# First attention of a two-block model: another order for VectorE's row maxima, taps, halves and weight splits, and two modulation rows taken ahead of the exponentials

## The reference

```python
def hybrid_mixer(h, w_in, b_f, conv_w, conv_b, conv_ln_g, conv_ln_b, w_o):
    q, k, v, f_logit, conv_val, conv_gate = jnp.split(h @ w_in, splits, axis=-1)
    log_f = jax.nn.log_sigmoid(f_logit + b_f)
    attn = fox_attention(q, k, v, log_f)          # 8 heads of 64, causal, softmax over rows
    u = conv_val * jax.nn.sigmoid(conv_gate)
    u = causal_depthwise_conv(u, conv_w, conv_b)  # 31 taps, 512 channels
    u = jax.nn.silu(layer_norm(u, conv_ln_g, conv_ln_b))
    return jnp.concatenate([attn, u], axis=-1) @ w_o

# fox_attention, per block of 128 queries:
#   s = q k^T / sqrt(64) + cum[t] - cum[s], masked to s <= t;  p = softmax(s);  out = p v
# ahead of it: mod = silu(c) @ ada_w + ada_b (shifts, scales and gates of every norm)
# after it: x + g1 * rms_norm(y), then a SwiGLU feed-forward, then the second block
```

## Time and profile before

| | us |
|---|---|
| median of three runs | 1454.34 |
| the profiled execution: its time | 1453.96 |
| its span, first to last instruction | 1452.2 |
| TensorE busy, of the span | 1364.5 |
| VectorE busy | 820.9 |
| ScalarE busy | 589.0 |
| GpSimd busy | 409.3 |
| mean granted TensorE clock | 0.967 of full |

### The profile page before, as it was taken

The page is one execution under the profiler, slowest core; times in us unless marked ns, Lnnn a source line. Parts: engine busy times, 40 slices in busy tenths (PEclk is TensorE's granted clock), DMA queues, the critical chain, the costliest instruction groups (busy, mean ns, idle before and its releaser), DMA issues. The chain is left out here.

```text
span 1452.2 us, 19530 instructions
## 1 busy us (share of the span) xinstructions
PE 1364.5 (94%) x7904; PEld 1080.3 (74%) x7904; DVE 820.9 (57%) x965; ACT 589.0 (41%) x848; POOL 409.3 (28%) x191
## 2 busy tenths in 40 slices
PE   5999789969999999999999998998999999999996
PEld 3777566748888888887778886766777799777775
DVE  3788763476556555333755665776842831565544
ACT  4323445442222222212454346776632422455541
POOL 0000000018987888999200000000000050232220
PEclk9999889979999999999799999999999999999998
DMA  9433035213544545554132333334132342111121
GB/s 390 148 145 117 30 109 182 66 51 120 215 186 166 186 167 222 204 182 174 58 120 87 114 109 105 117 102 151 38 110 88 127 163 88 58 47 42 59 88 58
DMA packets 41350, 181.12 MB, mean 125 GB/s; under 512 B 3392, under 2 KB 20160, under 8 KB 21312
## 3 DMA queue, kind: packets, MB, share of 16 engines
q1 hardware_dynamic: 40128, 171.73, 32.9%
q10 hardware_dynamic: 1152, 8.39, 1.7%
HBM read 173.75 MB, written 6.36 MB: 124 GB/s over the span
## 5 line engine op out<-in xcount | busy, mean ns | idle before, releaser
L193 DVE TENSOR_TENSOR wlo<-raw,whi 128x2048 fp32r<-128x2048 f32 x95 | 253.7, 2670 | 182.2 <-ACT whi L189 179.6
L200 POOL TENSOR_TENSOR ada_raw<-ada_raw,cs 128x2048 f32<-128x2048 f32 x36 | 150.1, 4171 | 504.2 <-DVE h2lo L451 457.5
L271 PE MATMUL ps<-hhi,whi 128*128 128x512 f32 x640 | 252.1, 394 | 2.3 <-PEq L562 0.8
L271 PE MATMUL ps<-hhi,wlo 128*128 128x512 f32 x640 | 249.4, 390 | 0.0
L271 PE MATMUL ps<-hlo,whi 128*128 128x512 f32 x640 | 249.1, 389 | 0.0
L189 ACT ACTIVATE whi<-raw 128x2048 fp32r<-128x2048 f32 x95 | 181.5, 1911 | 143.6 <-PE ps L1303 91.3
L209 POOL TENSOR_TENSOR ada_raw<-ada_raw 128x1024 f32<-128x1024 f32 x72 | 164.4, 2283 | 5.7
L271 PEld LDWEIGHTS ps<-hhi,whi 128*128 128x128 f32 x640 | 120.2, 188 | 28.7 <-issue 2.4
L271 PEld LDWEIGHTS ps<-hhi,wlo 128*128 128x128 f32 x640 | 120.1, 188 | 25.7
L271 PEld LDWEIGHTS ps<-hlo,whi 128*128 128x128 f32 x640 | 120.2, 188 | 24.3
L2030 POOL TENSOR_TENSOR x<-x,rest 128x256 f32<-128x256 f32 (+3 forms) x32 | 49.0, 1531 | 163.8 <-DVE rest L2325 163.8
(11 more groups left out here) (373 smaller groups left out, 2810.1 us busy)
## 6 DMA issues: line engine op xcount, KB each, us to landing
raw<-panels SPq DMA_DIRECT2D x87, 1024.0 KB, 4.9
ada_raw<-ada SPq DMA_DIRECT2D x48, 1024.0 KB, 6.7
first<-ada SPq DMA_DIRECT2D x8, 1024.0 KB, 20.7
bc<-ac_rows SPq DMA_DIRECT2D x32, 256.0 KB, 3.8
raw<-panels ACTq DMA_DIRECT2D x8, 1024.0 KB, 5.1
x_kept<-x SPq DMA_DIRECT2D x2, 2048.0 KB, 9.6
x<-x_kept SPq DMA_DIRECT2D x2, 2048.0 KB, 8.0
x<-x_in SPq DMA_DIRECT2D x1, 2048.0 KB, 9.1
```

Of the source, the lines that this page charges most:

```text
L193: e.tensor_tensor(wlo[:, c % 2, :, :], raw[:, c % 2, :, :], whi[:, c % 2, :, :].bitcast(F32), ALU.subtract).then_inc(lo_split, 1)
L200: e.tensor_tensor(ada_raw[:, c % 2, :, :], ada_raw[:, c % 2, :, :], cs[:, which, :].unsqueeze(2).to_broadcast([P, KT, 256]), ALU.mult).the ...
L271: mm = e.matmul(ps[:, 2 * (qc % 2) + b, :], w[:, c % 2, 2 * k + b, :], src[part][:, k, :], **flags)
```

## The change

It reorders one block's programs and adds no arithmetic:

- In dense step 5, VectorE writes `ncx` ahead of the step's ten taps, not behind them.
- In dense step 6, the split of panel 8 is taken out; it now follows the row maximum of unit 0.
- In the units, VectorE's row maximum and the reciprocal come first; then `out_lo`; then a split if one is due (`SPLIT_AT`: panels 8, 9, 10, 11 in units 0, 7, 9, 12); then the taps; and last `take_half`, which no longer splits.
- On ScalarE, in units 11 and 12, the first `ada_keep` comes ahead of the exponentials. Units 13 and 14 stay.

```diff
@@ ScalarE, units @@
                             if n >= 7 and n % 4 == 3:
                                 out_hi((n - 7) // 4)
+                            if n in (11, 12):
+                                ada_keep(act, ROWS_AT[n][0], MODB, 256)
                             if n < NU:
...
-                            if n in ROWS_AT:
+                            if n in (13, 14):
                                 ada_keep(act, ROWS_AT[n][0], MODB, 256)
@@ VectorE, dense steps @@
-                            split_lo(dve, s + 2, 0)
+                            if s < DENSE - 1:
+                                split_lo(dve, s + 2, 0)
...
-                            conv_taps(dve, done_taps, done_taps + DENSE_TAPS[s])
-                            done_taps += DENSE_TAPS[s]
                             if s == 5:
                                 dve.wait_ge(A["nc_hi"], 2)
                                 for r0 in (0, HD):
                                     dve.tensor_tensor(ncx[r0 + 32:r0 + 32 + H1, :], ncum,
                                                       ncx[0:H1, :].bitcast(F32), ALU.subtract).then_inc(A["nc"], 1)
+                            conv_taps(dve, done_taps, done_taps + DENSE_TAPS[s])
+                            done_taps += DENSE_TAPS[s]
@@ VectorE, units @@
-                            if b == 1:
-                                split_lo(dve, c + 2, 0)
+
+                        SPLIT_AT = {0: DENSE + 1}
+                        SPLIT_AT.update({n + 1: HALVES[H][1] + 2 for n, H in HALF_AT.items() if HALVES[H][2] == 1})
...
                         for n in range(NU + 3):
-                            if n >= 7 and n % 4 == 3:
-                                out_lo((n - 7) // 4)
                             if n < NU:
                                 dve.wait_ge(A["s_done"], n + 1)
...
-                            if n in HALF_AT:
-                                take_half(HALF_AT[n])
+                            if n >= 7 and n % 4 == 3:
+                                out_lo((n - 7) // 4)
+                            if n in SPLIT_AT:
+                                split_lo(dve, SPLIT_AT[n], 0)
                             if n == 15:
                                 read_mod(dve, 8, 20)
...
+                            if n in HALF_AT:
+                                take_half(HALF_AT[n])
```

## The result

The changed kernel takes 1438.01 us, the median of four runs (1437.19 to 1440.56); beside them the kernel before took 1453.96 us. The ratio is 0.9888, with a 95% interval of 0.9873 to 0.9902, so 16 us are gone, clear of noise. The forecast was 1437.5 us, in a range of 1429 to 1446.

A forecast was written before the change was run, and what follows sets the result against it. TensorE was held up by VectorE, late by order, not load, in the first attention's units. Terms -20.0 (waits), +3.0 (half clock) and +0.6 (end) sum to -16.4 us from 1453.96: 1437.5 us, range 1429 to 1446.

The forecast's parts named there:

- Start: Before unit 0: ncx ends at 120.4, not 127.1, so unit 0's logits start 1.56 us earlier, at 125.8.
- Units 0 to 4: New 2.6 us idle before the second maximum, then halves no longer wait; unit 4's logits at 145.7, 3.8 us ahead.
- Units 4 to 8: TensorE is the bound again: four units in 21.3 us, unit 8's logits at 167.0, 11.1 us ahead.
- close meeting: Unit 8: panel 9's split ends about 167.7, v pieces need it at 168.0; priced at nothing, up to 1 us if late.
- Units 8 to 12: 26.4 us, kept-row waits of 0.4 and 1.1 replacing 3.48; unit 12's logits at 193.4, 20.0 us ahead.
- Units 12 to 15: Load a16 goes out behind w13, TensorE idles 2.8 us; 23.5 us in all, unit 15's logits at 216.9.
- Half clock: TensorE at 1.2 GHz: 7 of 28 us reached the end before; 3 us of the 7 left after the change.
- the walk: Stepping the engines' programs unit by unit at full clock; the old order gives unit 15's logits at 230, trace 236.94.
- End: Unit 15: read_mod now stands behind out_lo(2), adding 0.6 us to TensorE's existing 1.56 us wait.
- the lower bound: No half clock, a16 in time, units 2 us shorter: stated as -24.5 us, 1429.5 us.
- the rivals: Half clock stays or grows (chance 0.13), loads become the bound (0.06), waits move and nothing comes (0.04), slower (0.03).
- The loads: Rival: every row of units 12 to 14 waits for its load, some 3 x 2 us more, 1442 to 1447; chance 0.06.

The follow-up runs named there:

- half_only: Kernel before, with only take_half and its split of the next panel moved behind the taps: 1439.78 us, ratio 0.9899.
- half_back: Changed kernel with take_half put back ahead of the taps, the splits staying one unit later: 1446.07 us, ratio 0.9947.
- start_back: Changed kernel with the old start, ncx behind the ten taps and panel 8's split ahead of the first row maximum: 1437.73 us, ratio 0.9887.
- max_back: Changed kernel with out_lo ahead of the row maximum and splits of panels 9 to 11 right behind their halves: 1440.91 us, ratio 0.9915.
- keep_only: Kernel before, with only the first kept modulation row of units 11 and 12 ahead of ScalarE's exponentials: 1450.42 us, ratio 0.9968.
- keep_back: Changed kernel with the first kept rows of units 11 and 12 behind the exponentials again: 1440.41 us, ratio 0.9911.
- w13_late: Changed kernel with panel w13 moved behind a19 in SyncE's load list: 1438.16 us.
- taps_later: Changed kernel with three taps moved from unit 0 to units 11 to 13: 1435.63 us, ratio 0.9877.
- three_mended: Changed kernel with three taps moved to units 11 to 13, panel w13 behind a19, and read_mod ahead of out_lo(2): 1431.14 us, ratio 0.9853.
- max_only: Kernel before, with only out_lo behind the row maximum and splits of panels 9 to 11 behind the maximum one unit later: 1450.02 us, ratio 0.9965.

## Why the prediction was right

The forecast was 16.4 us under the profiled execution and 16.8 were measured there (16 between medians). Starts depend on where unit 0 lies, so here is the time from one unit's logits to another's, in us:

| from the logits of unit ... to ... | 0 to 4 | 4 to 8 | 8 to 12 | 12 to 15 | all |
|---|---|---|---|---|---|
| before | 22.2 | 28.5 | 35.3 | 23.6 | 109.6 |
| forecast, without half clock | 19.9 | 21.3 | 26.4 | 23.5 | 91.1 |
| changed kernel | 21.4 | 21.1 | 25.9 | 24.8 | 93.2 |
| half_only | 19.3 | 23.2 | 29.7 | 22.5 | 94.7 |
| half_back | 23.0 | 23.8 | 28.9 | 23.8 | 99.5 |

By its steps:

1. *Start.* 125.8 forecast, 125.67 measured, and the wait at the start is gone. But it brings nothing that can be measured: start_back is as fast as the whole.
2. *Units 0 to 4.* The logits of unit 1 at 129.7 (129.71), the second maximum at 134.2 (134.25), unit 2 at 135.9 (136.04) after 2.6 us idle (2.40). Unit 3 then came at 141.93, not 140.4, and unit 4 at 147.08, not 145.7: a stretch at half clock followed that wait, which step 6 priced separately.
3. *Units 4 to 8.* 21.3 us forecast, 21.12 measured. The close meeting of the split with the v pieces held. The place of the halves brings most of it (half_only 23.2 us, before 28.5); the last 2 us come with `out_lo` and the splits, whose wait of 2.0 us at unit 8 stands in half_only and in max_back. In between, in units 5 to 7, TensorE waits for nothing.
4. *Units 8 to 12.* 26.4 forecast, 25.85 measured. Of the two short waits, 1.13 us is there and the one of 0.4 shows in no row of the timeline. That the kept rows matter is shown by keep_only, 3.6 us, and by the trace of keep_back, 2.2 us in this stretch.
5. *Units 12 to 15.* 23.5 forecast without clock, 24.8 measured with 7 us of half clock. The mechanism is shown: w13 went out at 197.91, a16 behind it, and without w13 there the wait is gone (w13_late). Its size was overdrawn, 1.15 us for 2.8. The load took 7.9 us and not 6.9, but TensorE, slowed in unit 12, wanted it 11 us after the logits of unit 12 and not 8.4. In taps_later, at full clock there, it lands 6.9 us after its issue and TensorE waits 2.60 us, nearly the forecast's case. One reading of rows 7 was wrong: w13 did not have the queue to itself before, it went out 0.38 us behind a15 and took 8.1 us to land.
6. *Half clock.* I left 3 of 7 us, reading from the rows that idle times over 2 us bring it and shorter ones don't; that reading did not hold (below). Beyond the walk, units 0 to 4 took 1.5 us more, and units 12 to 15, with the wait for a16 taken at its measured length, 3.0 us more: some 4.5 us at the places where the clock was down, for the 3 that were left. The wait for a16, 1.65 us shorter than forecast, and units 4 to 12, 0.7 us shorter, paid that back, so that the logits of unit 15 came at 218.85 against 219.9. The terms were right in kind; that the sum fits within about 1 us is in part luck. The Trainium skill, page "TensorE: Matmul & The Clock Gate", section "HAM oscillation — how this bites in real kernels", would take half of the throttled time as its price; for the 28 - 13 = 15 us at half clock that went, that rule gives an estimate of 7.5 us. The traces speak for less: by the walk 7 us were lost of the 24 at half clock up to unit 15 in the kernel before, and some 4.5 of 10 in the changed one, so 2.5 came back. The timed runs agree. For each run, 2 x (1 - mean clock) x span is its time at 1.2 GHz in the whole kernel. Over the 54 runs of the kernel before beside the experiments this is 90 to 117 us, and a run's time rises by 0.23 us for each us of it (correlation 0.79); 15 us at that price are 3.4 us, an estimate. The four to twelve runs of each other kernel are few for a price of their own.
7. *End.* The wait for `read_mod` went from 1.56 to 2.16 us, the 0.6 forecast, and back to 1.56 in three_mended.

Two sums outside the forecast are off by a little: the lower bound adds up to -24.2, not -24.5, and 76 us in place of 50 are 26 more, not 27. Neither touches the range.

Of the rivals, none came, and none of the signs of being wrong. The loads did not become the bound, though they are the next to: at the faster pace of taps_later they take back part of the gain. What the prediction did not say, and would have been worth saying, is how unevenly the gain is spread. It told the parts in order of time; by the runs the call of `take_half` carries 14.3 us alone (with its splits) and 8.1 when only it is put back, `out_lo` and the splits 4.0 and 2.9, the kept rows 3.6 and 2.4, the start 1.4 and nothing. Of these, 2.9, 2.4 and 1.4 are not clear of nothing. One overlap is seen in the traces: the wait of 3.61 us at unit 4's values is gone in half_only and cut to 1.22 in max_only. That the other overlaps are of this kind is my reading, not shown.

Open: which part of the 14.3 us of half_only is clock. An estimate: its six runs have a mean clock of 0.970, the 25 of the kernel before beside them 0.9645, so some 17 us less at 1.2 GHz, 4 us at the price of 0.23; with the walk's 10.8 that makes 14.8. Open too is what brings the half clock in unit 12.

## What to carry to other kernels

An engine that is busy for 60% can be what everybody waits for, if its in-order program has a wait for another engine ahead of work that needs no wait. Put the work that is ready (here the taps) ahead of the instruction that waits, and the result others wait for (the maximum) ahead of both. Then look at what the moved step feeds on a third queue: here the later split held a panel's load in SyncE's list, and through it a load that TensorE needed; moving that panel, three taps and one read gave 7 us more.

## What the runs showed of the hardware

The clock was less regular than I had read it. In the kernel before, a wait of 1.56 us at the first logits brought no half clock (mean clock 1.00 from 128 to 132 us); in half_only the same wait was followed by a mean clock of 0.57 from 128 to 132 us. The wait of 2.40 us in unit 1 was followed by a mean clock of 0.83 from 136 to 146 us in the changed kernel, and by full clock in the same stretch of keep_back, the same instructions up to there:

```profile
136.00:146.00 10.00, 8.50 (x48) 6.44 (x49) 10.00 (x18) 4.70 (x15) 0.00 (x0) 1.00 0.55 233
```

Runs of one kernel differ with it: w13_late ran at 1433 to 1434 us twice, with a mean clock of 0.971, and at 1438 to 1439 three times, with 0.968 to 0.969. Also, the logits of unit 0 started anywhere from 125.63 to 129.09 us in kernels whose program up to there differs by 1.56 us at most; a shift of one place between two profiles is better read from one landmark to the next than from the span's start.

A load of 1 MB landed 4.8 us after its issue where nothing had gone out just before it (w13 in the changed kernel), and 6.9 to 8.1 us where another 1 MB load had gone out 0.4 us earlier (w13 in the kernel before 8.1, a16 in the changed kernel 7.9, in max_only 7.1, in taps_later 6.9).
